# Multiplying the identity by itself ahead of eleven steps of a one-core four-layer kernel

## The chip, the core and the metric

The kernel runs on one core of one Trainium2 chip. The metric is the device time of one execution, in microseconds (us). Three runs of the kernel before took 941.01, 941.76 and 944.14 us; the median is 941.76. Beside TensorE (PE in the profile; its weight loads are PEld) the core has VectorE (DVE), ScalarE (ACT), GpSimd (POOL) and SyncE (SP). Each engine has its own instruction stream, and semaphores tie them together.

## The reference, cut to what matters

One sequence of 256 positions, 1024 wide, goes through four layers in float32:

```
even: h = rms_norm(x);  dsa attention (top-k indexer) | retention;  @ w_out; x += rms_norm(.)
odd:  h = rms_norm(x);  differential attention | latent attention;  @ w_out; x += rms_norm(.)
a:    NSA attention + memory attention, @ w_out, layer_norm(ALPHA*x + .), conv_ffn, layer_norm
b:    MoBA attention + memory attention, @ w_out, layer_norm(ALPHA*x + .), conv_ffn, layer_norm
```

All weights, some 140 MB, are used once per execution. What matters here is that a layer can begin only when the norm at the end of the one before it is done, first for rows 0 to 127 (q = 0), then for rows 128 to 255 (q = 1).

## The kernel before, in words

Each product of activations and weights is done in three passes over a high and a low half of both operands (`whi`/`wlo`, `thi`/`tlo`), each of a reduced type with one pass through TensorE. ACT makes the high half of a weight unit (`act_split`, L646) and DVE the low half (`dve_split`, L652). The units of 128 x 1024 come by DMA from SP's queue.

The order of the work is written out by hand as lists of steps: `START`, `EVEN`, `ODD`, `NSA`, `feed(l)` and `MOBA`. Every engine walks the same lists and does its part of each step. The steps that matter here, as TensorE sees them:

- `("T", k, q)` is `pe_rows_t`: two banks of four transposes each (L732) turn the rows of half q of the layer's input. It waits for the norm (`hrow`, or `xw`). ACT and DVE then make `thi` and `tlo` from the banks (L739, L746).
- `("chunk", name, k, q)` is `pe_chunk` (L701 to L703): rows of half q times unit k of a matrix, accumulated in one bank over the units. It waits for `tlo`.
- `("tile", name, t)` is `pe_tile` (L684 to L686): 24 matmuls for 128 output columns and all 256 positions.
- `("log", g)` is `pe_log` (L871): the attention scores of group g into banks 4 and 5. DVE masks them and finds the maximum (L984), ACT takes the exponentials (L997), and DVE's `("mul", g)` scales them (L1015, or L1030 and L1035).
- `("turn", g, side)` is `pe_turn` (L880): transposes of the scaled scores, waiting for `mul`. ACT and DVE copy them out. `("val", g)` (L923, L927) multiplies them with the values, and after it ACT and DVE make two halves of the result (L956, L962).
- `("proj", s, n, q)` is `pe_project` (L791): unit n of the output matrix, for half q. With n of 7 it ends the sum, and the norm follows.
- `("ret", k)` is the retention (L1362 to L1371): scores of head k, and values of head k - 1.

At each change of layer the order is: `proj` 4 to 7 for q = 0, `proj` 4 to 6 for q = 1, `T` for q = 0, `proj` 7 for q = 1, the first chunks for q = 0, `T` for q = 1, then the chunks for q = 1. The groups are numbered through: 0 to 2 are dsa, 3 to 5 mla, 6 to 8 diff, 9 and 10 memory, 11 to 19 NSA, 20 to 26 the last attention layer.

`Engine.fill(bank, ...)` waits until what the bank held has been read. Between it and the wait for a step's data stands a call of `pe_keep`, which multiplies the identity by itself into the bank, as often as the table `KEEP` says for that step. In the kernel before the table is empty, so nothing is issued. `pe_warm` (L710 to L713) issues the same multiplication at the start of the program, 16 times at each of two calls, where TensorE waits for its first data.

The functions that read the table:

Of the kernel before, what the change touches and what calls it, by code (L numbers as in the profile page):

```python
# [16 lines left out]
T = 256  # L17
# [214 lines left out]

KEEP = {}


class Group:
# [23 lines left out]
def _build(nc, ctx, inp, out_dram, plan):  # L262
# [452 lines left out]
    def pe_keep(p, bank, *step, at=0):  # L715

        for _ in range(KEEP.get(step, 0)):
            p.i.matmul(ps[:, bank, at:at + P], ident[:, :], ident[:, :], start=True, stop=True)
# [55 lines left out]
    def pe_project(p, s, n, q, residual):  # L774
        u = U[f"{s}_out"][n]
        if ("proj", s, n, q) in KEEP:
            p.fill(7)
# [1583 lines left out]
```

How the kernel before makes its waits and increments, by code:

```python
    def wait_ge(self, topic, *key):  # L213
        t = self.tally
        if t.sems is None:
            return
        v = t.at[topic, key] if key else t.count.get(topic, 0)
        if v > self.seen.get(topic, 0):
            self.i.wait_ge(t.sems[topic], v)
            self.seen[topic] = v
# [5 lines left out]
    def fill(self, bank, *emptied_by):  # L227
        for step in self.emptied.get(bank, ()):
            self.wait_ge(*step)
        self.emptied[bank] = emptied_by
# [382 lines left out]
    def sp_loads(s, units):  # L614
        for u in units:
            j, n = split_no[u], plan[u]["len"]
            if j >= NRAW:
                s.wait_ge("hi", split_units[j - NRAW])
                s.wait_ge(*lo_of(split_units[j - NRAW]))
            src = inp["ws"][plan[u]["at"]:plan[u]["at"] + P * n].rearrange("(p n) -> p n", p=P)
            s.i.dma_start(raw[:, j % NRAW, 0:n], src).then_inc(*s.sig(f"raw{j % NRAW}", u, by=16))
# [1 line left out]
    def act_w1_load(a, i):  # L623
        if i < 4:
            a.wait_ge("mix_t", "o", 3)
        elif i < 6:
            a.wait_ge("xw", "o", 1, 1)
        else:
            a.wait_ge("w1", w1_units[i - 6])
        at = plan[w1_units[i]]["at"]
        a.i.dma_start(w1_bufs[i % 6], inp["ws"][at:at + P * UNIT].rearrange("(p n) -> p n", p=P)).then_inc(*a.sig(f"w1raw{i}", "all", by=16))
# [7 lines left out]
    def act_split(a, upto):  # L640
        for u in due(a, upto):
            j, n = split_no[u], plan[u]["len"]
            a.wait_ge(f"raw{j % NRAW}", u)
            if j >= NSPLIT:
                a.wait_ge(*used(split_units[j - NSPLIT]))
```

## Time and profile before

| | |
|---|---|
| runs | 941.01, 941.76, 944.14 us; median 941.76 |
| the profiled execution, its own time | 941.11 us |
| its span, first to last instruction | 939.3 us |
| TensorE busy | 901.2 us (96%) |
| weight loads | 774.3 us (82%) |
| VectorE busy | 650.4 us (69%) |
| ScalarE busy | 489.0 us (52%) |
| mean granted TensorE clock | 0.988 of full speed |

Busy TensorE time is modelled: a matmul's record is longer than the distance to the next, as they overlap. Where a cost is worked out, the distance from one start to the next is what counts. A clock of 1.00 is the full 2.4 GHz, 0.50 is 1.2 GHz.

### The profile page before, as it was taken

Reading aid. Unit: us, or ns where it says so; the run is one execution under the profiler, and the core shown is the slowest. Engines: PE = TensorE matmul, PEld = TensorE weight load, DVE = VectorE, ACT = ScalarE, POOL = GpSimd, SP = SyncE. Lnnn points to the kernel's source line nnn. Section 1 sums busy time; section 2 is a strip of 40 time slices with the busy share of each in tenths; the row PEclk is TensorE's granted clock in tenths of the full one; section 3 lists DMA queues with packets and bytes.
Section 4 is the critical chain, followed back from the end, with each engine's and each line's share of the span. In section 5 each row is a group of like instructions: output and inputs, shape, how many; then the busy total and the mean of one; then the engine's idle time right before and its main releaser. Section 6 shows DMA issues by size and latency. Waiting matters only on the chain.

```text
span 939.3 us, 14616 instructions
## 1 busy us (share of the span) xinstructions
PE 901.2 (96%) x5650; PEld 774.3 (82%) x5650; DVE 650.4 (69%) x1182; ACT 489.0 (52%) x890; POOL 41.5 (4%) x73
## 2 busy tenths in 40 slices
PE   8999999899998899999999999998999999999997
PEld 8888987688986788767888888887897788888885
DVE  5659585756666646857697678676664778768676
ACT  5454274456666456644455454544654455455441
POOL 2005000100001100000000000000000000000000
PEclk9999999989999999999999999999999999999999
DMA  8845434364362752111656655547242356555561
GB/s 310 297 143 166 153 113 141 129 224 158 113 198 77 285 188 91 68 46 68 202 179 202 189 196 179 186 169 244 94 156 95 131 202 222 184 190 184 186 202 45
DMA packets 45504, 155.06 MB, mean 165 GB/s; under 512 B 5404, under 2 KB 8060, under 8 KB 45436
## 3 DMA queue, kind: packets, MB, share of 16 engines
q1 hardware_dynamic: 40688, 141.78, 44.6%
q10 hardware_dynamic: 4748, 12.36, 4.1%
q8 instruction: 45, 0.74, 0.3%
q14 instruction: 23, 0.19, 0.1%
HBM read 152.78 MB, written 1.34 MB: 164 GB/s over the span
## 4 chain that ended last, share of the span: by engine, by line
PE 82%; DVE 9%; ACT 5%; issue 1%; POOL 1%; DMA 1%; DVEq 0%; ACTq 0%; SPq 0%
PE ps L2035 16%; PE ps L2050 13%; PE ps L791 7%; PE ps L2034 7%; PE ps L684 5%; PE ps L685 5%; PE ps L686 5%; PE ps L701 4%; PE ps L703 3%; PE ps L702 3%; PE ps L871 3%; PE ps L880 2%; PE ps L923 2%; DVE wlo L652 2%; PE ps L803 1%
## 5 line engine op out<-in xcount | busy, mean ns | idle before, releaser
L652 DVE TENSOR_TENSOR wlo<-raw,whi 128x1024 fp32r<-128x1024 f32 (+1 forms) x263 | 313.5, 1215 | 30.6 <-ACT whi L646 30.1
L646 ACT ACTIVATE whi<-raw 128x1024 fp32r<-128x1024 f32 (+1 forms) x263 | 271.3, 1046 | 90.4 <-DMA raw<-in_ws 36.7
L2035 PE MATMUL ps<-t,whi 128*128 128x512 f32 x640 | 221.6, 396 | 0.0
L2034 PE MATMUL ps<-t,wlo 128*128 128x256 f32 x560 | 156.2, 279 | 0.0
L684 PE MATMUL ps<-t,whi 128*128 128x256 f32 (+1 forms) x480 | 140.4, 293 | 0.3 <-ACT arena L1665 0.3
L685 PE MATMUL ps<-t,whi 128*128 128x256 f32 (+1 forms) x480 | 136.5, 284 | 0.0
L686 PE MATMUL ps<-t,wlo 128*128 128x256 f32 (+1 forms) x480 | 136.4, 284 | 0.0
L2035 PEld LDWEIGHTS ps<-t,whi 128*128 128x128 f32 x640 | 115.9, 188 | 22.5
L2034 PEld LDWEIGHTS ps<-t,wlo 128*128 128x128 f32 x560 | 105.6, 189 | 3.6
L2050 PE MATMUL ps<-whi,r 128*128 128x512 f32 x352 | 98.0, 390 | 0.0
L684 PEld LDWEIGHTS ps<-t,whi 128*128 128x128 f32 (+1 forms) x480 | 92.3, 192 | 6.4 <-issue 4.3
L685 PEld LDWEIGHTS ps<-t,whi 128*128 128x128 f32 (+1 forms) x480 | 92.4, 193 | 0.2
L686 PEld LDWEIGHTS ps<-t,wlo 128*128 128x128 f32 (+1 forms) x480 | 92.3, 192 | 0.0
L701 PE MATMUL ps<-whi,t 128*128 128x512 f32 (+3 forms) x208 | 77.9, 375 | 6.7 <-DVE t L746 4.7
L2050 PEld LDWEIGHTS ps<-whi,r 128*128 128x128 f32 x352 | 66.1, 188 | 13.1
L702 PE MATMUL ps<-wlo,t 128*128 128x512 f32 (+3 forms) x208 | 74.7, 359 | 0.0
L703 PE MATMUL ps<-whi,t 128*128 128x512 f32 (+3 forms) x208 | 74.7, 359 | 0.0
L997 ACT ACTIVATE sm<-sm,stat 128x128 f32<-128x128 f32 (+1 forms) x92 | 40.4, 441 | 28.8 <-DVE stat L984 28.8
L2050 PE MATMUL ps<-wlo,r 128*128 128x512 f32 x176 | 54.8, 389 | 0.0
L701 PEld LDWEIGHTS ps<-whi,t 128*128 128x128 f32 x208 | 40.5, 195 | 16.9 <-issue 10.9
L2148 DVE TENSOR_TENSOR r<-arena,r 128x512 fp32r<-128x512 f32 x22 | 15.2, 692 | 48.2 <-ACT r L2094 48.2
L2094 ACT ACTIVATE r<-arena 128x512 fp32r<-128x512 f32 x22 | 13.9, 632 | 62.8 <-PE ps L2050 58.4
(268 smaller groups left out, 1280.7 us busy)
## 6 DMA issues: line engine op xcount, KB each, us to landing
raw<-in_ws SPq DMA_DIRECT2D x256, 512.0 KB, 4.1
vecs<-in_vecs ACTq DMA_DIRECT2D x12, 512.0 KB, 6.1
arena<-in_ws ACTq DMA_DIRECT2D x5, 512.0 KB, 6.6
raw<-in_ws SPq DMA_DIRECT2D x4, 384.0 KB, 3.5
tb<-brow ACTq DMA_DIRECT2D x8, 192.0 KB, 5.4
rows<-in_mem SPq DMA_DIRECT2D x2, 512.0 KB, 4.0
x<-in_x SPq DMA_DIRECT2D x1, 1024.0 KB, 10.1
rows<-in_ws ACTq DMA_DIRECT2D x2, 512.0 KB, 7.6
```

The source lines that it names most:

```text
L646: a.i.activation(whi[:, j % NSPLIT, 0:n], raw[:, j % NRAW, 0:n], ACT.Copy).then_inc(*a.sig("hi", u))
L652: d.i.tensor_tensor(wlo[:, j % NSPLIT, 0:n], raw[:, j % NRAW, 0:n], whi[:, j % NSPLIT, 0:n].bitcast(F), ALU.subtract).then_inc(*d.sig("lo" ...
L684: p.i.matmul(ps[0:m, b, 0:T], wh[:, k, :], thi[:, k, :], start=k == 0, stop=False)
L685: p.i.matmul(ps[0:m, b, 0:T], wh[:, k, :], tlo[:, k, :], start=False, stop=False)
L686: mm = p.i.matmul(ps[0:m, b, 0:T], wl[:, k, :], thi[:, k, :], start=False, stop=k == 7)
L701: p.i.matmul(ps[:, b, 0:n], xh, wh[:, kl, :], start=k == 0 and kl == 0, stop=False)
L702: p.i.matmul(ps[:, b, 0:n], xh, wl[:, kl, :], start=False, stop=False)
L703: mm = p.i.matmul(ps[:, b, 0:n], xl, wh[:, kl, :], start=False, stop=final and kl == nk - 1)
L791: mm = p.i.matmul(ps[:, 2 * q + z, :], x_, w_[:, 0, 512 * z:512 * z + 512], start=n == 0 and y == 0 and not residual, stop=n == 7 and y == 2)
L2034: p.i.matmul(ps[:, b, 0:T], wl[:, k, :], thi[:, k, :], start=False, stop=False)
L2035: mm = p.i.matmul(ps[:, b, :], wh[:, k, :], t2[:, k, :], start=k == 0, stop=k == 7)
L2050: mm = p.i.matmul(ps[:, 2 * q + n, :], g_, w_[:, 0, 512 * n:512 * n + 512], start=False, stop=final and y == 2)
```

## The change

The table gets eleven entries: a step, and how many multiplications of the identity TensorE issues ahead of it, once the bank is free and before it waits for the step's data. They add up to 81. Nothing else differs; the results of the added multiplications are overwritten by the step.

```diff
-KEEP = {}
+KEEP = {('T', 5, 1, 0): 6, ('proj', 'e', 4, 1): 8, ('ret', 0): 12,
+        ('log', 19): 8, ('turn', 17, 0): 3, ('T', 3, 0, 0): 8,
+        ('chunk', 'a_v', 1): 4, ('T', 3, 1, 0): 12, ('turn', 12, 1): 4,
+        ('chunk', 'e_av', 1): 12, ('log', 12): 4}
```

The helper that reads it, which is in both kernels:

```
    def pe_keep(p, bank, *step, at=0):
        for _ in range(KEEP.get(step, 0)):
            p.i.matmul(ps[:, bank, at:at + P], ident[:, :], ident[:, :], start=True, stop=True)
```

`("T", k, q, b)` is bank b of the step `T k q`; `("ret", 0)` stands in the step `ret 1`, ahead of head 0's values; `("chunk", name, q)` stands ahead of the first unit for half q. `("proj", "e", 4, 1)` also waits there for bank 7, which its own step does not use.

## Rows read from the trace of the kernel before

**Rows 1.** The page: span, and busy time by engine.
```profile
span 939.3 us, 14616 instructions
PE 901.2 (96%) x5650; PEld 774.3 (82%) x5650; DVE 650.4 (69%) x1182; ACT 489.0 (52%) x890; POOL 41.5 (4%) x73
```
**Rows 2.** The page: the chain that ended last, by engine.
```profile
PE 82%; DVE 9%; ACT 5%; issue 1%; POOL 1%; DMA 1%; DVEq 0%; ACTq 0%; SPq 0%
```
**Rows 3.** Windows: stretch, length, busy PE PEld DVE ACT POOL, PEclk, DMA share, GB/s.
```profile
186.32:193.15 6.83, 5.94 (x20) 5.57 (x21) 4.75 (x7) 2.55 (x4) 0.00 (x0) 0.50 0.59 157
288.72:292.13 3.41, 3.32 (x16) 3.35 (x17) 0.00 (x0) 0.49 (x1) 0.00 (x0) 0.50 0.00 0
326.27:333.09 6.82, 6.82 (x34) 6.82 (x34) 2.25 (x6) 1.15 (x2) 0.00 (x0) 0.50 0.50 184
442.32:445.73 3.41, 3.41 (x11) 2.83 (x10) 2.70 (x4) 2.92 (x5) 0.00 (x0) 0.50 0.00 0
```
**Rows 4.** Timeline of PE, chunks, `T 3 1`, chunks: start, us, what, idle before, releaser.
```profile
183.57 0.33 PE L702 MATMUL ps<-wlo,t 128*128 128x384 f32 x1
183.74 0.34 PE L703 MATMUL ps<-whi,t 128*128 128x384 f32 x1
186.56 1.97 PE L732 MATMUL ps<-ident,rows 128*128 128x128 f32 x8 [2.48 <-DVE rows L1135]
189.18 0.66 PE L701 MATMUL ps<-whi,t 128*128 128x384 f32 x1 [0.65 <-DVE t L746]
...
190.28 0.52 PE L701 MATMUL ps<-whi,t 128*128 128x384 f32 x1
190.60 0.52 PE L702 MATMUL ps<-wlo,t 128*128 128x384 f32 x1
```
**Rows 5.** Timeline of PE: the second call of `pe_warm`, at the start.
```profile
9.34 3.74 PE L713 MATMUL ps<-ident 128*128 128x128 f32 x32
```
**Rows 6.** Timeline of PE: `T 1 1`, chunk `e_av` for q = 1, and `iw`.
```profile
42.35 1.03 PE L732 MATMUL ps<-ident,rows 128*128 128x128 f32 x8
44.59 0.47 PE L701 MATMUL ps<-whi,t 128*128 128x512 f32 x1 [1.20 <-DVE t L746]
...
61.03 0.28 PE L1334 MATMUL ps<-ident,arena 4*128 4x4 f32 x2 [2.15 <-ACT arena L1399]
```
**Rows 7.** Timeline of PE: the values of head 0 in `ret 1`.
```profile
97.23 0.49 PE L1362 MATMUL ps<-arena,sm 128*128 128x128 f32 x2
```
**Rows 8.** Timeline of PE: `T 3 0`.
```profile
177.13 0.95 PE L732 MATMUL ps<-ident,rows 128*128 128x128 f32 x7 [1.86 <-DVE rows L1135]
```
**Rows 9.** Timeline of PE: `T 5 1` and chunk `a_v` for q = 1.
```profile
321.86 1.32 PE L732 MATMUL ps<-ident,x 128*128 128x128 f32 x8 [1.20 <-DVE x L1149]
324.95 0.31 PE L701 MATMUL ps<-whi,t 128*128 128x164 f32 x1 [1.77 <-DVE t L746]
```
**Rows 10.** Timeline of PE: `log 12`, then `turn 12 0` and `turn 12 1`.
```profile
370.40 1.13 PE L871 MATMUL ps<-arena 64*128 64x256 f32 x8
379.71 1.06 PE L880 MATMUL ps<-ident,arena 128*128 128x128 f32 x8 [1.00 <-DVE arena L1015]
```
**Rows 11.** Timeline of DVE: the mask of `log 12`.
```profile
371.97 0.42 DVE L984 CUSTOM_DVE_ANT_0 arena<-ps,tb 128x256 f32<-128x256 f32 x1
```
**Rows 12.** Timeline of PE: `log 19`, `proj a 4 1`.
```profile
420.25 1.14 PE L871 MATMUL ps<-arena 64*128 64x256 f32 x8
422.45 0.50 PE L791 MATMUL ps<-whi,t 128*128 128x512 f32 x1 [1.07 <-DVE t L962]
```
**Rows 13.** Timeline of ACT: the high half that `proj a 4 1` needs.
```profile
421.82 0.26 ACT L956 ACTIVATE t<-ps 128x128 fp32r<-128x128 f32 x1
```
**Rows 14.** Timeline of PE: `turn 7`, between `turn 6` and `turn 8`.
```profile
286.94 0.66 PE L880 MATMUL ps<-ident,sm 128*128 128x128 f32 x4 [2.26 <-DVE sm L1035]
```
**Rows 15.** Waits of all engines: line, waited for, us in total, times, longest.
```profile
DVE sm L984 <- PE ps L871: 21.6, 13, 4.9
```
**Rows 16.** Windows of line 713 alone: stretch, length, busy PE PEld, PEclk, DMA, GB/s.
```profile
3.41:5.41 2.00, 2.00 (x11) 2.00 (x11) 1.00 1.02 379
```

## The prediction

> **What bounds the kernel now.** I read the page first: span 939.3 us, TensorE busy 901.2 of it [rows 1]. Then the chain that ended last, 82% of it TensorE [rows 2]: what TensorE issues more, or issues at half clock, goes to the end unless it lies in a wait. Third, the windows in which the granted clock was low [rows 3]: after the start and before the end it stood at 0.50 (1.2 GHz) in four stretches, from 186.32, 288.72, 326.27 and 442.32 us on, together 20.5 us, in which TensorE was busy for 19.5. Last, the timeline of TensorE at the eleven places, to see how long it waits there and for whom.
>
> How a wait is read: the bracket counts from the modelled end of the last matmul, which overlaps the next. A matmul that lasts 0.33 us is followed by the next after 0.17 [rows 4], so TensorE could have issued 0.16 us sooner than the bracket says. I add 0.16 to each bracket.
>
> **The price of one multiplication.** The 16 of one call of `pe_warm` leave 32 records, two for each, in 3.74 us with some 0.28 for the last one's own length [rows 5]: 3.46 / 31 = 0.112 us a record, 0.223 us a multiplication at full clock. So 81 cost 18.1 us of TensorE's time. The question is how much of it lies in waits that end for another reason.
>
> The Trainium skill ("TensorE: Matmul & The Clock Gate", section "Wait — 56ns, not 53.3ns?") gives about 56 ns for a bf16 matmul of 128 columns at 2.4 GHz. By that the 81 would cost an estimated 4.5 us, nearly all of it inside waits. No row here is of bf16; the rows of the float32 identity itself show four times that, and the trace decides.
>
> **Part by part, in program order.** Over = multiplications less wait.
> - `chunk e_av 1`: 12 are 2.68 us, its wait is 1.20 + 0.16 = 1.36 [rows 6]: 1.32 over. The next wait of TensorE, at `iw`, is for ACT's copy of TensorE's own last tile, so it moves along [rows 6].
> - `ret 0`: 12, 2.68 us, and the row has no wait at all [rows 7]: 2.68 over.
> - `proj e 4 1`: 8, 1.79, has no wait itself, but `T 3 0`, three `proj` later, has one of 2.02 us [rows 8]. Its releaser hangs on the q = 0 sum alone, which is done before `proj e 4 1`, so this wait takes them in. `T 3 0` adds 8 more, 1.79. Together 3.57 against 2.02: 1.55 over. Behind it on TensorE stands `proj e 7 1`, and the norm of q = 1 and `T 3 1` hang on that.
> - `T 3 1`: 12, 2.68, against 2.64 [rows 4]: 0.04 over.
> - `T 5 1`: 6, 1.34, against 1.36; `chunk a_v 1`: 4, 0.89, against 1.93 [rows 9]. Nothing over. The cover is DVE's work on the norm and on `tlo`; without it they would cost 2.23.
> - `log 12`: 4, 0.89, no wait. Its scores are done at about 371.5, DVE masks them from 371.97 [rows 10, 11], and up to `turn 12 0`, which waits for L1015, DVE is the late one. So 0.5 is absorbed and 0.4 over; bounds 0 and 0.89. `turn 12 1`: 4, 0.89, follows `turn 12 0` in one unbroken row [rows 10]: 0.89 over.
> - `turn 17 0` (3) and `log 19` (8): 2.45, no wait of their own. The next step, `proj a 4 1`, needs two halves of an earlier group; ACT makes the high one at 421.82, behind exponentials of an earlier `log` [rows 13], so its wait of 1.23 [rows 12] takes in as much: 1.22 over.
>
> Sum: 1.32 + 2.68 + 1.55 + 0.04 + 0.4 + 0.89 + 1.22 = 8.1 us. Bounds: 18.1 if every wait hangs on TensorE and moves in full, 3.0 if waits further on take in most of the first five places (the first rival).
>
> **What the clock gives back.** The fall at 186.32 comes during the wait for `T 3 1`, the one at 326.27 just behind the waits of `T 5 1` and `chunk a_v 1` [rows 3, 4, 9]. With the identity running TensorE has hardly a pause there, and I take both as gone.
> - In the first, eight transposes and the way to the chunk take 2.62 us (186.56 to 189.18) against 2.24 around `T 1 1` at full clock [rows 4, 6]: 0.3. Twelve chunk matmuls stand 0.32 apart (190.28, 190.60) where others stand 0.17 apart [rows 4]: 1.8. Together 2.1.
> - In the second TensorE is busy in all of the 6.82 us [rows 3]: half of it, 3.4.
>
> Sum 5.5 us. The falls at 288.72 and 442.32 are not at a step of the table; I leave them in, 1.7 us each (half of 3.41). Bounds: 0 if no fall goes, 8.9 if all four do.
>
> Where the clock falls need not be the same in each execution, and this is one. The three runs, 3.1 us apart, would fit one or two falls more or less. The Trainium skill (the same page, section "Part 1: The HAM clock gate (the "warmup" mystery)") calls the point of the transition variable from run to run; one trace cannot show it.
>
> **Forecast.** 941.11 + 8.1 - 5.5 = 943.7 us, made against the profiled execution's own time (span 939.3 and 1.8 around it). That execution lies 0.65 below the median of 941.76. I let 943.7 stand as the median after, 0.2% above the median before.
>
> **The rivals.**
> - *The delays are taken in before the end (faster).* `turn 6` to `turn 8` wait for DVE's L1035, 2.26 us at `turn 7` alone [rows 14]. If that DVE work were late for its own reasons, it would take in about 5.1 us of the first five places' 5.6: cost 3.0, time 941.11 + 3.0 - 5.5 = 938.6. It is below the median before from 2 us absorbed on. Against it: DVE itself waits for TensorE's scores, 21.6 us in 13 waits at L984 [rows 15], so it should move along.
> - *The clock gains nothing (slower).* The identity doesn't hold the clock, or the shifted order falls at other waits instead, as at `iw`. Cost 8.1 alone: 949.2; with the larger of the two falls merely moved, 941.11 + 8.1 - 2.1 = 947.1. For it: most waits get no identity. Against it: in a cold stretch of 2 us with only these multiplications there were 11 records [rows 16], soon after they stood 0.112 apart, so the clock rose under them.
> - *The later falls go too.* The shift moves one of them away: 942.0; both: 940.3.
> - *The multiplications are cheap.* At the columns per us of the chunks, 384 in 0.17 [rows 4], 128 take 0.057. Then only `ret 0` (0.7) and `turn 12 1` (0.2) are over: 941.11 + 0.9 - 5.5 = 936.5. [Rows 5] speak against it. The page's 56 ns would say the same.
>
> **How the numbers follow.** A measurement of this kernel tells about 0.3%, 2.8 us, from no change: below 938.9 is faster, above 944.6 slower. The forecast with its own range, 941.5 to 945.5, gets 0.50 (0.35 of it same, 0.15 slower); the absorbed delays 0.14 (0.11 faster, 0.03 same); the clock without gain 0.20 (slower); the later falls gone 0.13 (0.10 same, 0.03 faster); the cheap multiplication 0.03 (faster). Faster 0.17, same 0.48, slower 0.35. The range of 8 in 10 goes from 939.5 to 947.5: under it lie the absorbed delays and the cheap multiplication, over it the clock without any gain.
>
> **What would show it.** In the profile after: 162 records of TensorE at the line in `pe_keep`, 0.112 us apart. The values in `ret 1` start 2.7 us behind the tile before them. `T 3 0` starts about 5.6 us later than before, and `o_lora` for q = 1 has steps of 0.17 at clock 1.00. After `T 3 1`'s layer begins the kernel is 3.4 us behind, after the tile `a_c 0` level, and at the first FFN 2.5 us behind. I am wrong if `proj o 0 0` starts less than 2 us later than before (absorbed), if the windows there still show 0.50, or if new low windows stand elsewhere.

## The result and the profile after

| | before | after |
|---|---|---|
| runs, same chip | 941.88 us (940.26 to 944.16, 20 runs) | 943.92 us (942.91 to 945.57, 20 runs) |
| profiled execution, own time | 941.11 us | 943.47 us |
| its span | 939.3 us | 941.7 us |
| mean granted clock | 0.988 | 0.995 |

The ratio is 1.0018, with a 95% interval of 1.001 to 1.0026. The ratio weighs all the runs and is not the quotient of the two medians: by it the kernel became 1.7 us slower, by the medians 2.0. That is less than the 0.3% that was taken as the bound for "the same"; the twenty runs on each side still tell it from nothing. 943.7 had been forecast.

The page of the kernel after, first span and busy time, then the clock by slices and the chain by engine:

```profile
span 941.7 us, 14936 instructions
PE 912.8 (97%) x5812; PEld 788.0 (84%) x5812; DVE 650.6 (69%) x1182; ACT 489.5 (52%) x890; POOL 41.5 (4%) x73
PEclk9999999999998999999999999999999999999999
PE 86%; DVE 8%; ACT 4%; issue 1%; POOL 0%; DMA 0%; DVEq 0%; ACTq 0%
```

TensorE is busy 11.6 us longer than in [rows 1], and its share of the chain went from 82% to 86% [rows 2]. The other engines did the same work in the same time. In the line of slices one is at 8, the thirteenth; the line before had one too, the ninth. Short falls hardly show there, so the clock is read from windows.

Windows of the kernel after (columns as in [rows 3]). The first is the only one outside start and end with a low clock; the other three are where the clock fell before:

```profile
290.99:297.81 6.82, 5.99 (x27) 5.62 (x28) 1.73 (x7) 3.21 (x15) 0.24 (x2) 0.50 0.13 50
184.00:200.00 16.00, 14.79 (x94) 13.94 (x93) 12.32 (x17) 10.49 (x24) 2.54 (x6) 1.00 0.59 204
324.00:336.00 12.00, 11.21 (x95) 10.77 (x95) 7.92 (x15) 5.95 (x10) 2.98 (x8) 1.00 0.70 223
442.00:450.00 8.00, 6.39 (x40) 4.29 (x39) 7.00 (x12) 4.16 (x6) 0.79 (x2) 1.00 0.19 67
```

So 20.5 us at 1.2 GHz became 6.8. If that were all, the kernel would be some 6.8 us faster.

The new instructions, one line of the source view (least, median and greatest duration in ns, first and last start):

```profile
L721 PE MATMUL ps<-ident x162: 270/275/308, 44.3 to 425.4; 128*128 128x128 f32 x162
```

The timeline of TensorE in the kernel after, at the table's places (start, us, what, idle before and its releaser; lines stand 3 higher than before):

```profile
44.32 2.84 PE L721 MATMUL ps<-ident 128*128 128x128 f32 x24
46.92 0.48 PE L704 MATMUL ps<-whi,t 128*128 128x512 f32 x1
...
63.34 0.22 PE L1337 MATMUL ps<-ident,arena 4*128 4x4 f32 x1 [2.15 <-ACT arena L1402]
...
99.36 0.28 PE L689 MATMUL ps<-t,wlo 128*128 128x256 f32 x1
99.48 2.84 PE L721 MATMUL ps<-ident 128*128 128x128 f32 x24
102.16 0.39 PE L1365 MATMUL ps<-arena,sm 128*128 128x128 f32 x2
...
181.72 1.95 PE L721 MATMUL ps<-ident 128*128 128x128 f32 x16
183.50 0.27 PE L735 MATMUL ps<-ident,rows 128*128 128x128 f32 x1
...
190.25 2.84 PE L721 MATMUL ps<-ident 128*128 128x128 f32 x24
192.93 0.31 PE L735 MATMUL ps<-ident,rows 128*128 128x128 f32 x1
...
195.73 0.33 PE L704 MATMUL ps<-whi,t 128*128 128x384 f32 x1
195.90 0.33 PE L705 MATMUL ps<-wlo,t 128*128 128x384 f32 x1
...
288.15 0.66 PE L883 MATMUL ps<-ident,sm 128*128 128x128 f32 x4 [1.03 <-DVE sm L1038]
291.06 1.12 PE L883 MATMUL ps<-ident,sm 128*128 128x128 f32 x4 [2.26 <-DVE sm L1038]
...
329.53 0.35 PE L704 MATMUL ps<-whi,t 128*128 128x164 f32 x1 [0.79 <-DVE t L749]
```

What to see: where a bracket stood in [rows 4, 6, 8], there are now multiplications of the identity and no bracket. The 24 records at 44.32 take 2.60 us to the next matmul and the 24 at 99.48 take 2.68, 0.11 a record. In `ret` there was no bracket to begin with [rows 7], and the values stand 2.80 us after the last matmul of the tile. Two waits kept their length to a hundredth, 2.15 us at `iw` (63.34) and 2.26 at `turn 7` (291.06) [rows 6, 14]: what TensorE waits for there hangs on TensorE itself. And the chunks behind `T 3 1` stand 0.17 apart (195.73, 195.90), where they stood 0.32 apart.

**The ledger.** The delay of the same instruction, after against before, and what it grew by:

| stretch | predicted | found |
|---|---|---|
| start of the program | | +1.10 |
| `chunk e_av 1` | +1.32 | +1.21 |
| `ret 0` | +2.68 | +2.51 |
| `proj e 4 1` with `T 3 0` | +1.55 | +1.53 |
| `T 3 1`, the fall behind it gone | +0.04 - 2.1 | -2.21 |
| `turn 6` to `turn 8`, fall of 6.83 us instead of 3.41 | 0 | +0.55 |
| `T 5 1`, `chunk a_v 1`, the fall behind them gone | -3.4 | -3.16 |
| `log 12` | +0.4 | +0.52 |
| `turn 12 1` | +0.89 | +0.88 |
| `turn 17 0`, `log 19` | +1.22 | +1.31 |
| small differences between | 0 | -0.28 |
| `T 7 0`, no fall | 0 | -1.61 |
| up to the end | | +0.05 |

The places with a count in the table add up to 7.96 us, the two falls that went to -5.37, together +2.6 us. What stands at no place of the table is +1.10 + 0.55 - 1.61, nearly nothing. At the start of the program both kernels issue the same 32 records of the identity at a low clock, and the clock rises in between: they stand 0.21 us apart at first and 0.11 later, and took 5.17 us in the trace before and 6.23 after. The clock column can't be used for this stretch. It prints 1.00 in [rows 16], from 3.41 to 5.41, where the records stand 0.21 apart; the profile has no clock entry there yet. The next fence is from before, the one behind it from after:

```profile
2.58 5.17 PE L713 MATMUL ps<-ident 128*128 128x128 f32 x32 [2.58 <-DMA ident<-in_ident]
```

```profile
2.64 6.23 PE L716 MATMUL ps<-ident 128*128 128x128 f32 x32 [2.64 <-DMA ident<-in_ident]
```

### The profile page after: what moved, and what is told of

Read it like the earlier page. It is cut to its first block, busy times and chain, and to the rows that moved or that the text cites. A ratio compares the mean times of both kernels' runs of the same rounds, so it can differ in the third digit from the quotient of the medians.

```text
span 941.7 us, 14936 instructions
## 1 busy us (share of the span) xinstructions
PE 912.8 (97%) x5812; PEld 788.0 (84%) x5812; DVE 650.6 (69%) x1182; ACT 489.5 (52%) x890; POOL 41.5 (4%) x73
## 4 chain that ended last, share of the span: by engine, by line
PE 86%; DVE 8%; ACT 4%; issue 1%; POOL 0%; DMA 0%; DVEq 0%; ACTq 0%
PE ps L2038 16%; PE ps L2053 13%; PE ps L794 8%; PE ps L2037 7%; PE ps L687 5%; PE ps L688 5%; PE ps L689 5%; PE ps L704 4%; PE ps L705 4%; PE ps L706 4%; PE ps L874 3%; PE ps L883 2%; PE ps L926 2%; DVE wlo L655 2%; PE ps L806 1%; PE ps L721 1%
## 5 line engine op out<-in xcount | busy, mean ns | idle before, releaser
L687 PEld LDWEIGHTS ps<-t,whi 128*128 128x128 f32 (+1 forms) x480 | 91.3, 190 | 6.4 <-issue 4.3
L688 PEld LDWEIGHTS ps<-t,whi 128*128 128x128 f32 (+1 forms) x480 | 91.5, 191 | 0.2
L704 PE MATMUL ps<-whi,t 128*128 128x512 f32 (+3 forms) x208 | 76.6, 368 | 5.0 <-DVE t L749 3.0
L706 PE MATMUL ps<-whi,t 128*128 128x512 f32 (+3 forms) x208 | 73.2, 352 | 0.0
```

What stands on the lines that cost most here:

```text
L687: p.i.matmul(ps[0:m, b, 0:T], wh[:, k, :], thi[:, k, :], start=k == 0, stop=False)
L688: p.i.matmul(ps[0:m, b, 0:T], wh[:, k, :], tlo[:, k, :], start=False, stop=False)
L704: p.i.matmul(ps[:, b, 0:n], xh, wh[:, kl, :], start=k == 0 and kl == 0, stop=False)
L706: mm = p.i.matmul(ps[:, b, 0:n], xl, wh[:, kl, :], start=False, stop=final and kl == nk - 1)
```

## The experiments

The theory: each multiplication costs 0.22 us less the wait in which it lies, and gives something back only where it fills a pause behind which the clock falls. A first rival: the gain comes from all places, the identity keeping TensorE busy in general. A second: the places without a wait cost less than their count says, because delays are taken in before the end. Each ratio is to runs of the kernel before on the same chip. The runs of before lie in two groups, near 941.2 and near 944 us, so a median jumps with the number of runs in each, and the ratio is the safer of the two.

### The covered entries alone

```diff
-KEEP = {}
+KEEP = {('T', 3, 1, 0): 12, ('T', 5, 1, 0): 6, ('chunk', 'a_v', 1): 4}
```

> Only T 3 1 (12), T 5 1 (6) and chunk a_v (4) keep their multiplications, the three that lie in waits. Theory (a multiplication costs 0.223 us less the wait it lies in; the two falls of the clock there go): 5.5 less than before, 936.4 against the 941.9 us of before, a ratio of 0.994; no window under 1.00 at 186 to 193 and at 326 to 333. Rival 'the clock gains nothing, the falls only move': 941 to 942, ratio 1.000. Rival 'the gain in the profile after came from elsewhere, as its start and its last fall differ too': anything, but the stretch from T 3 1 to tile a_c 1 would not shrink by 5.

938.22 us (935.49 to 940.45, 8 runs), ratio 0.995 (0.9931 to 0.9968), with 936.4 and 0.994 expected. The profiled execution took 940.45, the most of the eight. Its windows:

```profile
184.00:200.00 16.00, 14.48 (x87) 12.91 (x86) 11.99 (x25) 10.04 (x21) 3.13 (x7) 1.00 0.64 229
287.41:294.24 6.83, 5.82 (x29) 5.45 (x28) 1.38 (x4) 3.11 (x15) 0.64 (x2) 0.50 0.08 32
320.00:334.00 14.00, 13.21 (x113) 12.77 (x112) 8.87 (x18) 7.90 (x13) 3.22 (x8) 1.00 0.68 224
382.98:386.39 3.41, 3.41 (x5) 1.35 (x4) 2.26 (x6) 3.41 (x14) 0.00 (x0) 0.50 0.00 0
441.01:444.42 3.41, 3.41 (x13) 3.03 (x14) 2.29 (x5) 2.08 (x4) 0.00 (x0) 0.50 0.02 5
```

Behind `T 3 1` and behind `T 5 1` the clock stays at 1.00, and the trace gained 2.2 and 3.2 us there, as in the full change. But this execution also fell at 62.13 (the wait of `iw`) and at 382.98, where the first trace of before did not, and at 441.01 (`T 7 0`), where it did. The first of these cost 1.5 us in the trace, the second 1.7. The clock of each run tells the same: three runs near 935.5 had 0.995, four from 937.8 to 939.0 had 0.992 or 0.993, and the one at 940.45 had 0.989. The covered entries do nearly all the good, and how much of it is seen hangs on which other falls an execution has.

### The other eight entries alone

```diff
-KEEP = {}
+KEEP = {('proj', 'e', 4, 1): 8, ('ret', 0): 12, ('log', 19): 8, ('turn', 17, 0): 3, ('T', 3, 0, 0): 8, ('turn', 12, 1): 4, ('chunk', 'e_av', 1): 12, ('log', 12): 4}
```

> The other eight places alone (59 multiplications, 13.2 us). Theory: 8.1 us over their waits, and all falls of the clock stay: 950.0, ratio 1.0085. Rival 'part of the delay is taken in before the end': up to 5 less, 945 to 947. Rival 'these places hold the clock too, in executions in which it falls there': 947 or less.

949.4 us (947.74 to 950.13, 6 runs), ratio 1.0073 (1.0055 to 1.009). 950.0 and 1.0085 had been expected. By the medians it is 8.1 us over 941.34, just what had been worked out for these places; by the ratio it is 6.9, with an interval from 5.2 to 8.5, so the exact agreement is luck. In the trace the delays come in at their places, 1.2 at `e_av` and 2.5 at `ret`, and nothing is taken in before the end (+8.7, with some 0.95 of it from the start of the program). Its profiled execution had four low windows of 20.5 us in all, as before, one of them longer:

```profile
328.27:338.51 10.24, 8.74 (x41) 8.37 (x41) 4.60 (x10) 3.67 (x6) 2.19 (x6) 0.50 0.60 190
```

The first rival is out: eight places with 59 multiplications gave back nothing. So is the second: it allowed 3.0 us for all the places, and the interval begins at 5.2. The two halves also add up to the whole. By the ratios they are -4.7 us (-6.5 to -3.0) and +6.9, their sum +2.2, and the whole change is +1.7. The medians, -3.1 and +8.1, would make +5.0 of it, but that is the two groups of runs and no effect between the halves.

### The change without the entry of `ret`

Against the changed kernel:

```diff
-KEEP = {('T', 5, 1, 0): 6, ('proj', 'e', 4, 1): 8, ('ret', 0): 12,
+KEEP = {('T', 5, 1, 0): 6, ('proj', 'e', 4, 1): 8,
...
```

> The changed kernel without the 12 ahead of the values of ret 1. Theory: 2.5 to 2.7 less than the changed kernel's 943.9, so 941.3, ratio 0.9995 against before. Rival 'the 12 hold the clock at some other place, or are absorbed': 943 to 944.

940.86 us (940.1 to 942.16, 12 runs), ratio 0.9986 (0.9973 to 0.9999). 941.3 had been expected. Against the whole change's 1.0018 it is 0.3%, 3.0 us (1.6 to 4.4), for a place whose 12 multiplications cost 2.5 in the trace. This one entry decides the sign of the change. Its profiled execution had a fall at the wait of `iw`, as the covered entries alone had:

```profile
63.76:67.17 3.41, 3.41 (x18) 3.41 (x17) 2.09 (x5) 0.02 (x1) 0.00 (x0) 0.50 0.46 153
```

### A table fitted to the waits

If the theory holds, a better table can be read off the trace: only places with a wait, and no more multiplications than the bracket holds, `turn 6` to `turn 8`, `T 7 0` and `iw` among them. At `iw` the wait for the bank stood behind the wait for the data, so the identity gets its place ahead of it.

```diff
-KEEP = {}
+KEEP = {('iw',): 10, ('chunk', 'e_av', 1): 6, ('T', 3, 0, 0): 9, ('T', 3, 1, 0): 11,
+        ('turn', 6, 0): 5, ('turn', 7, 0): 10, ('turn', 8, 0): 6, ('T', 5, 1, 0): 6,
+        ('chunk', 'a_v', 1): 8, ('T', 7, 0, 0): 7}
...
-                p.wait_ge("ev", "e_idx", 2)
                 p.fill(3, ("iw", 0))
+                pe_keep(p, 3, "iw")
+                p.wait_ge("ev", "e_idx", 2)
```

> Each long wait gets as many multiplications as fit in it, and nothing stands where there is no wait: chunk e_av 6, iw 10 (issued ahead of its wait for ACT's copy), T 3 0 9, T 3 1 11, turn 6 5, turn 7 10, turn 8 6, T 5 1 6, chunk a_v 8, T 7 0 7. Theory: no cost, and no fall of the clock from the start on, so before's four falls (2.1, 1.7, 3.4 and 1.7 us) come back whole: 941.1 - 8.9 = 932.2, up to 934 if one fall stays in some executions; ratio 0.990 to 0.992; the window list shows 1.00 from 8 us to the end. Rival 'only the two falls of e1 can be avoided': 936.4. Rival 'multiplications in a wait slow the DVE or ACT work that ends it': above 936.4, and the waits' ends later than in e1.

935.12 us (933.43 to 935.81, 6 runs), ratio 0.9922 (0.9905 to 0.9939): 78 multiplications, nearly as many as the 81 of the change, and 9 us away from it. 932.2, up to 934, had been expected, so it is a miss by 1 us at least. In its trace the delay against the first trace of before falls by 2.2 us at `T 3 1`, 1.1 at the turns, 3.2 at `T 5 1` and `chunk a_v 1` and 1.6 at `T 7 0`: 8.1 of the 8.9 forecast. The start of the program took back 0.6, and one low window 1.7. That window lies at no place of this table:

```profile
378.70:382.10 3.40, 3.40 (x8) 1.85 (x8) 2.18 (x6) 3.40 (x17) 0.00 (x0) 0.50 0.00 0
```

The timeline of TensorE ahead of it:

```profile
373.72 1.06 PE L880 MATMUL ps<-ident,arena 128*128 128x128 f32 x8 [1.02 <-DVE arena L1015]
375.86 2.84 PE L1812 MATMUL ps<-arena 128*128 128x32 f32 x24
378.53 0.95 PE L880 MATMUL ps<-ident,arena 128*128 128x128 f32 x4
```

This fall is not behind a wait like the others. The last bracket, of 1.02 us, ends 5.0 us ahead of it, and what stands just before it are 24 small matmuls of 32 columns each, issued without a pause. The windows at 382.98 in the covered entries and at 381.06 in a kernel further down begin behind the same 24 matmuls. A table fitted to waits has no entry for such a place. Of the fitted table's six runs three, at 935.3 to 935.8, have a granted clock of 0.997, as this one has, and the others, at 933.4 to 934.9, 0.998 or 0.999.

The timeline of this kernel at `T 3 0` and `T 3 1`:

```profile
175.75 2.06 PE L718 MATMUL ps<-ident 128*128 128x128 f32 x17
177.65 1.04 PE L732 MATMUL ps<-ident,rows 128*128 128x128 f32 x8
...
184.40 2.62 PE L718 MATMUL ps<-ident 128*128 128x128 f32 x22
187.06 1.10 PE L732 MATMUL ps<-ident,rows 128*128 128x128 f32 x8
```

The eight transposes of `T 3 1` start 0.5 us behind their place before (186.56, [rows 4]), as everything in this trace does from the program's start on, so the multiplications in the wait did not make DVE's work later. They take 1.10 us instead of 1.97.

### The same table with transposes

Is it the multiplication, or any instruction of TensorE? A transpose of the identity leaves one record where the multiplication leaves two, so each is replaced by two.

```diff
-            p.i.matmul(ps[:, bank, at:at + P], ident[:, :], ident[:, :], start=True, stop=True)
+            p.i.transpose(ps[:, bank, at:at + P], ident[:, :], ident[:, :])
```

with every count of the fitted table doubled.

> The table of e4, with two transposes of the identity in place of each multiplication, so that each wait is filled for nearly the same time (a transpose leaves one record, some 0.11 us, two make 0.22). Theory (the clock asks only that TensorE's columns flow, of whatever kind): as e4, 935, and one low window at most after 8 us. Rival, by the Trainium skill (TensorE: Matmul & The Clock Gate, section Part 4: PE-mode transpose), that transposes do not count for the clock as multiplications do: the falls of before come back and the time is before's, 941 to 942, with 0.50 in the windows at 184 to 191 and 320 to 327.

934.34 us (933.17 to 935.07, 5 runs), ratio 0.9916 (0.9903 to 0.993). In one window from the start to the end the clock is at 1.00:

```profile
8.40:930.00 921.60, 904.35 (x5781) 778.62 (x5780) 650.25 (x1182) 488.26 (x889) 40.46 (x66) 1.00 0.50 165
```

The transposes held the clock. The Trainium skill ("TensorE: Matmul & The Clock Gate", section "Part 4: PE-mode transpose") says that the clock gate doesn't open for transpose mode, as a transpose does not count as TensorE being busy in the same way. This window doesn't agree for float32 transposes, up to 22 in a row (2.6 us at `T 3 1`), and the measurement decides. It doesn't show that a transpose counts as much as a multiplication, since half the multiplications hold the clock too (next section). It doesn't show either that transposes alone would raise the clock from a cold start.

### Half and a quarter of the fitted counts

Does the wait have to be full? Half: 37 multiplications; a quarter: 15. The rest is as in the fitted table.

```diff
+KEEP = {('iw',): 5, ('chunk', 'e_av', 1): 3, ('T', 3, 0, 0): 4, ('T', 3, 1, 0): 5,
+        ('turn', 6, 0): 2, ('turn', 7, 0): 5, ('turn', 8, 0): 3, ('T', 5, 1, 0): 3,
+        ('chunk', 'a_v', 1): 4, ('T', 7, 0, 0): 3}
```

> The table of e4 with half the count at each step (chunk e_av 3, iw 5, T 3 0 4, T 3 1 5, turn 6 2, turn 7 5, turn 8 3, T 5 1 3, chunk a_v 4, T 7 0 3). Theory (what matters is that TensorE's pauses get shorter, not that none is left): within 1 us of e4's 935.1, few falls. Rival (a wait must be filled to its end): 938 to 942, the falls of before at the waits left half open.

> The kernel of e6 once more, as the reference for e12 and because e9 spread over 5 us. Theory A (half counts hold the clock wherever the waits fall): 933 to 935.5 again. Theory B (half counts hold it in some executions only, and e6's five were lucky): a spread of 3 us or more, median 935 to 937.

Half: 934.09 us (933.26 to 934.77, 5 runs), ratio 0.9918 (0.9903 to 0.9933), the lowest median of all. Once more on another chip: 934.15 (933.99 to 937.48, 6 runs), ratio 0.9924 (0.9907 to 0.9942). In the first profiled execution the clock stood at 1.00 throughout:

```profile
5.50:930.40 924.90, 898.19 (x5713) 771.98 (x5711) 650.16 (x1182) 488.58 (x890) 40.45 (x66) 1.00 0.50 166
```

But two of the six runs of the second measurement are at 937.4, 3.3 us above the other four, the size of one long fall or two short ones; their granted clock is 0.995, that of the four 0.998 or 0.999. So the median is that of theory A and the spread, 3.5 us, that of theory B. The fitted table's six lie within 2.4 us. From `turn 6` to `turn 8` the full counts gave back 1.1 us in the trace, the half counts 1.3: filled to the brim, these waits ran over by 0.2.

```diff
+KEEP = {('iw',): 2, ('chunk', 'e_av', 1): 1, ('T', 3, 0, 0): 2, ('T', 3, 1, 0): 2,
+        ('turn', 6, 0): 1, ('turn', 7, 0): 2, ('turn', 8, 0): 1, ('T', 5, 1, 0): 1,
+        ('chunk', 'a_v', 1): 2, ('T', 7, 0, 0): 1}
```

> The table of e6 halved once more: chunk e_av 1, iw 2, T 3 0 2, T 3 1 2, turn 6 1, turn 7 2, turn 8 1, T 5 1 1, chunk a_v 2, T 7 0 1. Theory (the clock follows how much TensorE does around a wait): with 0.2 to 0.5 us in waits of 1.2 to 2.6 some falls return, 935.5 to 939, most at the turns and at T 3 1. Rival (any activity in a wait is enough): as e6, 934.

A quarter: 938.36 us (937.56 to 940.64, 7 runs), ratio 0.9964 (0.995 to 0.9977). Three falls are back, at the same places as before:

```profile
187.10:193.93 6.83, 6.18 (x22) 5.80 (x21) 4.87 (x6) 2.81 (x4) 0.00 (x0) 0.50 0.68 201
286.09:292.92 6.83, 5.72 (x26) 5.43 (x27) 2.52 (x8) 3.35 (x12) 0.00 (x0) 0.50 0.24 77
327.05:330.46 3.41, 3.41 (x18) 3.41 (x18) 1.74 (x6) 1.15 (x2) 0.00 (x0) 0.50 0.71 281
```

This separates the two things that a count does. In a wait, fewer multiplications neither save nor cost time by themselves; with too few of them the fall comes.

### The two kernels once more

One more trace of each, to see which falls belong to a kernel and which to an execution.

> The kernel before, looked at once more. Theory that the falls are not the same in each execution: the low windows after the start are partly others than at 186, 289, 326 and 442, such as one at the wait of iw (60 to 66), and their cost accounts for the difference in time. Rival (the falls are fixed by the program): the same four windows.

> The changed kernel, looked at once more. Theory: no low window at 186 to 200 and 326 to 336, always one at the turns near 291, and one at T 7 0 (near 446) in some executions; the time 943 to 945.5. Rival (its one fall is fixed by the program): the same single window of 6.8 us.

The kernel before took 940.91 us, its low windows:

```profile
187.21:194.04 6.83, 6.18 (x23) 5.81 (x22) 4.93 (x6) 2.62 (x4) 0.00 (x0) 0.50 0.64 196
286.19:293.02 6.83, 5.06 (x23) 4.70 (x24) 2.63 (x9) 3.30 (x10) 0.00 (x0) 0.50 0.24 77
323.74:333.98 10.24, 8.65 (x40) 8.68 (x41) 3.90 (x10) 3.09 (x5) 1.55 (x6) 0.50 0.54 175
```

and none near 442. The first three falls of [rows 3] are of the kernel, longer or shorter by the execution (6.83, 3.41 and 6.82 us there; 6.83, 6.83 and 10.24 here); the fourth comes in some executions only: it is missing here, and there in the traces of the covered entries (441.01) and of the other eight (451.15). I had expected a fall at the wait of `iw` here, and there was none. More time at low clock (23.9 us for 20.5) did not make this execution slower: the start cost 0.5 more, the long third fall 0.9, and the missing fourth gave back 1.6.

The kernel after took 945.16 us, with the fall in the turns again and one at `iw`:

```profile
64.21:67.62 3.41, 3.41 (x18) 3.41 (x17) 2.10 (x5) 0.04 (x1) 0.00 (x0) 0.50 0.50 153
292.90:299.73 6.83, 5.66 (x28) 5.46 (x27) 1.21 (x4) 2.95 (x15) 0.81 (x2) 0.50 0.08 31
```

From 184 to 200 and from 324 to 336 the clock stood at 1.00 again. So the two gains repeat. The granted clock of every run bears that out beyond the two traces: all twenty runs of the changed kernel had 0.993 to 0.995, the 55 runs of the kernel before that were taken beside the experiments 0.983 to 0.990. The time is within the 943 to 945.5 expected, and no fall came at `T 7 0`. The fall at `iw`, which cost 1.5 us here and nothing in the first trace, is one of the things that make single runs differ. In a single trace it can't be told from an effect of the change.

### The entry of `ret` on top of the half counts, and of the fitted ones

If an uncovered entry costs its count, it costs it on any table. Against the half counts:

```diff
-        ('chunk', 'a_v', 1): 4, ('T', 7, 0, 0): 3}
+        ('chunk', 'a_v', 1): 4, ('T', 7, 0, 0): 3, ('ret', 0): 12}
```

> The table of e6, whose clock hardly falls, with the changed kernel's 12 ahead of the values of ret 1 on top. With the falls out of the way this prices a place without a wait alone. Theory: 12 x 0.223 less the 0.17 between two steps there, 2.5 us more than e6's 934.1: 936.6. Rival (work ahead of TensorE catches up later, so part is absorbed): 935 or less.

939.75 us (936.93 to 942.2, 10 runs), ratio 0.9968 (0.9954 to 0.9981). By the ratios (0.9968 - 0.9918) that is 0.5%, some 4.7 us, over the half counts, nearly twice what was expected: a miss. The step itself was 2.5 us longer in the trace, as it should be. That profiled execution had one low window, at 381.06, and a span of 935.5; the runs lie in groups at 937 and 939.9. With half counts a later fall comes in some executions (two of the six above), and the place of every pause had moved by 2.5 us. So the same entry was put on the full fitted table:

```diff
-        ('chunk', 'a_v', 1): 8, ('T', 7, 0, 0): 7}
+        ('chunk', 'a_v', 1): 8, ('T', 7, 0, 0): 7, ('ret', 0): 12}
```

> The full table of e4 with the 12 ahead of the values of ret 1. If e9's excess over 936.6 came from falls that half counts let through, the full counts take them away and the price of the place stands alone: e4's 935.1 + 2.5 = 937.6, spread 3 us at most. If the 12 cost more than their 2.5 us in themselves, it is 939 or more.

936.46 us (936.08 to 936.76, 5 runs), ratio 0.9936 (0.9923 to 0.9948), with 937.6 expected. On the same chip the half counts took 934.15: 2.3 us for the entry. Against the fitted table itself, measured on another chip, the ratios give 0.9936 - 0.9922 = 0.14%, 1.3 us, with intervals that leave anything from -0.7 to 3.3. The granted clocks say where the rest is: all five runs here had 0.999, three of the fitted table's six only 0.997. Against its other three, at 0.998 and 0.999, the entry costs some 2 us. In this kernel's trace the entry looks as it did in the change, and the clock never falls:

```profile
97.49 0.28 PE L686 MATMUL ps<-t,wlo 128*128 128x256 f32 x1
97.61 2.84 PE L718 MATMUL ps<-ident 128*128 128x128 f32 x24
100.29 0.39 PE L1363 MATMUL ps<-arena,sm 128*128 128x128 f32 x2
```

```profile
6.50:931.40 924.90, 908.18 (x5814) 783.20 (x5813) 649.89 (x1182) 489.04 (x890) 40.45 (x66) 1.00 0.50 165
```

The first of the two is the timeline, the second the window from start to end. What the half counts lost beyond 2.5 us was falls, by the granted clock of their ten runs with the entry: 936.93 us at 0.999, 937.2 and 937.3 at 0.997, six from 938.2 to 940.0 at 0.996, 942.2 at 0.994. The one at 0.999 lies 2.9 us above the median of the seven runs of the half counts at 0.998 or 0.999 (934.07, on other chips). Why falls came more often with the entry, the runs don't show.

## Why the prediction was right

**The price.** 0.112 us a record, 0.223 a multiplication [rows 5], held at every place (24 records in 2.60 to 2.68 us, 162 records in all). The cheap multiplication is out; the bf16 figure in the prediction did not carry over to a float32 operand.

**Multiplications less wait.** The six terms above 0.1 us came out within 0.17 us each, 7.96 against 8.06 in all. The largest miss is `ret 0` with 2.51 for 2.68. Its values stood 0.17 us behind the tile before and 2.80 after, which makes 2.63, and the second of them then follows the first by 0.22 us instead of 0.33. `log 12` was 0.52 for 0.4: DVE's late mask took in less than half of 0.89. That a wait on TensorE's own work moves along held to a hundredth of a microsecond at `iw` and `turn 7`, and it is why the absorbed delays did not come. DVE's wait at the scores [rows 15] was 22.4 us in 15 waits after, not shorter, in the line of the waits view:

```profile
DVE sm L987 <- PE ps L874: 22.4, 15, 4.9
```

**Long waits take in earlier work.** The 8 of `proj e 4 1` have no wait of their own, and were booked against that of `T 3 0`: 1.53 measured, 1.55 forecast. The same for `turn 17 0` and `log 19` against `proj a 4 1`: 1.31 and 1.22.

**What the clock gave back.** 5.37 against 5.5, in the two places named, and both repeat in the second trace. Halving the TensorE busy time of a low window (3.4 forecast, 3.16 found) and comparing the spacing of instructions at either clock (2.1 forecast, 2.2 found) served equally well.

**Right by a balance.** Three terms at no place of the table were not forecast: the start of the program +1.10, the longer fall in the turns +0.55, the absent fall at 442 -1.61. They cancelled to 0.04, and that is luck. The fall at 442 had been left in at 1.7 us as if it were of the kernel; the second trace of before doesn't have it, and three of the four traces of the kernels before and after are without it. The forecast compared the one profiled execution with the median and let the difference of 0.65 us stand. That is luck too: 943.7 is 0.2 us from the median, while the change itself was forecast as +2.6 and measured as +2.0 by medians and +1.7 by the ratio. The runs of before lie in two groups, and had the profiled one been of the slower, the traces' difference would have been off by some 3 us. What sets the groups apart is not shown; their granted clocks overlap (0.985 to 0.988 near 941.2, 0.983 to 0.986 near 944, on the first experiments' chip).

**What the prediction left out.** It knew falls only at waits. The one that cost the fitted table 1.7 us stood behind 24 small matmuls without a wait.

**The size.** 943.92 is 2.2 us above the median of the three runs, inside 0.3%, the case that had been given 0.48. The interval of the twenty runs, 1.0010 to 1.0026, leaves no doubt that it is slower all the same.

## What to carry to other kernels

Work put into a wait is free only up to the length of the wait; read the wait off the timeline, divide by the price of one instruction as this trace shows it, and put none where neither the row nor a wait soon behind it has room. A held clock is worth half of the TensorE busy time in the windows at half clock and no more, and only an entry in the pause at such a window earns it: here three entries earned 0.5%, eight others cost 0.7%, and a table fitted to the waits gave 0.8%, with half its counts as good in most executions. Before a fall of the clock is booked to a kernel, take a second trace, and compare the granted clock of all its runs.

## What the hardware showed that was not expected

- The clock fell at short pauses. In the first trace of before the fall at 186.32 came within the wait of 2.48 us that ended at 186.56 (`T 3 1`), and the one at 326.27 behind waits of 1.20 and 1.77 us, with TensorE busy again for 1.3 us. Not every pause does it: that of 2.15 us at `iw` was followed by a fall in three traces (without `ret`, the covered entries alone, the second of after) and by none in four (the two of before, the first of after, the other eight alone). What decides it between executions, no run here shows.
- It fell without a pause, too: behind 24 matmuls of 32 columns in 2.7 us, 5.0 us or more after the last wait, in three traces (378.70, 381.06, 382.98), while in the others it stayed up there.
- A wait need not be full. In the profiled execution with 5 multiplications ahead of `T 3 1` (10 records in 1.28 us) TensorE still waited 1.38 us behind them, and the clock stayed at 1.00; in the one with 2 it waited 2.05 us, and the clock was at 0.50 from 187.10 on:

```profile
184.10 0.61 PE L718 MATMUL ps<-ident 128*128 128x128 f32 x4
186.76 1.68 PE L732 MATMUL ps<-ident,rows 128*128 128x128 f32 x8 [2.05 <-DVE rows L1135]
```

That is the timeline of TensorE in the kernel with a quarter of the counts.
- The first rise of the clock comes sooner or later by the execution: the same 32 records took from 5.17 to 6.61 us in the fourteen traces, whose code up to there is the same. That alone makes up to 1.4 us between runs.
